# A streaming-encoder step on one core: the top-k rounds of the index attention as one list, 76 ahead of the first attention unit and 134 behind the reciprocals of group a's units

## The reference

```
shift, scale, gate = split(silu(c) @ w_ada + b_ada)
h = x * (1 + scale) + shift
qa, ka, va, ga, qb, kb, vb, gb, qi, ki, wi = split(h @ w_in)
oa = sliding-window attention(qa, ka, va, sinks, bias)            # group a, 16 heads
score = sum over 8 heads of relu(qi . ki / 8) * wi / sqrt(8)
idx = top_k(score, 256)                                           # 144 for the sample
ob = attention(qb, kb, vb) over the keys idx alone                # group b, 16 heads
y = concat(oa * silu(ga), ob * silu(gb)) @ w_out
out = LayerNorm(ALPHA * x + gate * y)
```

## Time and profile before

| | |
|---|---|
| median of 3 runs | 2170.78 us (2169.03 to 2174.48) |
| the profiled execution's own time | 2169.62 us |
| its span, first to last instruction | 2167.5 us |
| mean granted TensorE clock | 0.967 |
| busy share of the span | PE 92%, PEld 73%, DVE 45%, ACT 33%, POOL 28% |
| chain that ended last, by engine | PE 75%, DVE 10%, DMA 4%, ACT 4%, issue 3% |

### The profile page before, as it was taken

How to read it: one execution, slowest core, us unless ns; L and a number is a source line. 1 busy time by engine, 2 the same in 40 slices (tenths; PEclk the granted TensorE clock), 3 DMA queues, 4 the chain that set the end, 5 groups by cost and what they waited for, 6 DMA issues and landing times.

```text
span 2167.5 us, 34153 instructions
## 1 busy us (share of the span) xinstructions
PE 2003.6 (92%) x13111; PEld 1586.1 (73%) x13111; DVE 974.4 (45%) x2446; ACT 705.0 (33%) x1522; POOL 601.9 (28%) x607
## 2 busy tenths in 40 slices
PE   6889999959999999999899999999998889999991
PEld 3567789848888887888677777777776568777770
DVE  2433468876667776512223232232334422122447
ACT  2244422113233323333343434334435522221112
POOL 0331111112222222222222222222222434433333
PEclk8899999979999999999999999999999999999996
DMA  9943113312222222222211111111114134553443
GB/s 342 361 161 112 26 47 85 91 39 62 77 74 75 57 77 72 77 52 65 50 25 41 40 25 41 40 25 40 25 41 164 44 98 128 146 153 112 130 155 98
DMA packets 249922, 193.84 MB, mean 89 GB/s; under 512 B 149393, under 2 KB 202897, under 8 KB 247969
## 3 DMA queue, kind: packets, MB, share of 16 engines
q1 hardware_dynamic: 233072, 174.94, 28.2%
q10 hardware_dynamic: 15616, 12.49, 1.8%
q0 software_dynamic: 1072, 4.24, 0.6%
HBM read 171.28 MB, written 24.53 MB: 90 GB/s over the span
## 4 chain that ended last, share of the span: by engine, by line
PE 75%; DVE 10%; DMA 4%; ACT 4%; issue 3%; POOL 2%; SPq 1%; DVEq 0%; POOLq 0%; ACTq 0%
PE psum L1619 12%; PE psum L1621 10%; PE psum L1620 10%; PE psum L1697 6%; PE psum L1718 6%; PE psum L1719 5%; PE psum L1720 5%; PE psum L1655 5%; PE psum L1675 5%; DVE room L1202 4%; DVE room L1199 3%; DMA ada_ring<-in_w_ada_dram 2%; PE psum L1590 2%; PE psum L1546 2%; DMA w_raw<-in_w_out_dram 1%
## 5 line engine op out<-in xcount | busy, mean ns | idle before, releaser
L1619 PE MATMUL psum<-h_hi,w_hi 128*128 128x364 f32 (+1 forms) x1536 | 552.3, 360 | 6.7 <-issue 3.6
L1621 PE MATMUL psum<-h_lo,w_hi 128*128 128x364 f32 (+1 forms) x1536 | 507.2, 330 | 0.0
L1620 PE MATMUL psum<-h_hi,w_lo 128*128 128x364 f32 (+1 forms) x1536 | 504.2, 328 | 0.0
L1619 PEld LDWEIGHTS psum<-h_hi,w_hi 128*128 128x128 f32 x1536 | 290.3, 189 | 101.5 <-issue 96.1
L1081 POOL TENSOR_SCALAR room<-room 128x256 f32<-128x256 f32 (+9 forms) x252 | 149.0, 595 | 642.1 <-DVE room L1301 641.8
L1620 PEld LDWEIGHTS psum<-h_hi,w_lo 128*128 128x128 f32 x1536 | 292.2, 190 | 0.0
L1621 PEld LDWEIGHTS psum<-h_lo,w_hi 128*128 128x128 f32 x1536 | 290.3, 189 | 0.0
L1066 POOL TENSOR_TENSOR w_lo<-w_raw,w_hi 128x512 fp32r<-128x512 f32 x128 | 164.8, 1287 | 331.6 <-ACT w_hi L872 331.6
L1718 PE MATMUL psum<-w_hi,h_hi 128*64 128x512 f32 (+1 forms) x576 | 231.2, 401 | 14.1 <-POOL w_lo L1071 10.2
L1071 POOL TENSOR_TENSOR w_lo<-w_raw,w_hi 128x512 fp32r<-128x512 f32 x128 | 172.5, 1348 | 234.6 <-ACT w_hi L879 234.6
L1719 PE MATMUL psum<-w_lo,h_hi 128*64 128x512 f32 (+1 forms) x576 | 226.4, 393 | 0.0
(11 more groups left out here) (164 smaller groups left out, 2668.0 us busy)
## 6 DMA issues: line engine op xcount, KB each, us to landing
ada_ring<-in_w_ada_dram SPq DMA_DIRECT2D x64, 512.0 KB, 9.3
w_raw<-in_w_in_dram SPq DMA_DIRECT2D x256, 128.0 KB, 2.5
w_raw<-in_w_out_dram SPq DMA_DIRECT2D x256, 128.0 KB, 2.9
w_raw<-in_w_ada_dram SPq DMA_DIRECT2D x128, 128.0 KB, 2.1
x_rows<-in_x_prompt_dram SPq DMA_DIRECT2D x8, 1024.0 KB, 12.5
w_raw<-in_w_in_dram SPq DMA_DIRECT2D x32, 256.0 KB, 2.8
room<-in_x_prompt_dram SPq DMA_DIRECT2D x8, 1024.0 KB, 8.3
mix_transposed<-room SPq DMA_DIRECT2D x14, 544.0 KB, 3.0
```

Of the source, the lines that this page charges most:

```text
L1619: pe.matmul(Z, w_hi, hh[:, k, a:b], start=(k == 0), stop=False)
L1620: pe.matmul(Z, w_lo, hh[:, k, a:b], start=False, stop=False)
L1621: ins = pe.matmul(Z, w_hi, hl[:, k, a:b], start=False, stop=(k == KT - 1))
```

## The change

The two lists of rounds become one, `K_ROUNDS`, in the order of the tiles. 76 of its rounds run ahead of the first unit: all of tiles 2 and 3, and 12 of tile 4's. The other 134 are dealt out by `rounds_at(u)` over units 0 to 67: two to each unit, but one to units 33 and 67. All of a unit's rounds now stand behind its two reciprocals; none stands between the gate and the reciprocals any more. A tile's mask still follows its last round, and `mask_ready` follows the last round of all.

```diff
-K_EARLY = [2, 3, 4]
-K_LATE = [t for t in (5, 6, 7, 8) for _ in range((TOPK_P if t < NTILE - 1 else TOPK_S) // 8)]
-K_STEP = 2
+K_ROUNDS = [t for t in range(2, NTILE) for _ in range((TOPK_P if t < NTILE - 1 else TOPK_S) // 8)]
+K_EARLY = 76
+
+
+def rounds_at(u):
+
+    n, last = len(K_ROUNDS) - K_EARLY, 8 * STEPS - 4
+    return min(n, -(-n * (u + 1) // last)) - min(n, -(-n * u // last))
...
-        for t in K_EARLY:
-            for _ in range(TOPK_P // 8):
-                topk_round(t)
-            mask_of(t)
+        rounds = [0]
+
+        def topk_some(n):
+            for _ in range(n):
+                t = K_ROUNDS[rounds[0]]
+                topk_round(t)
+                rounds[0] += 1
+                if rounds[0] == len(K_ROUNDS) or K_ROUNDS[rounds[0]] != t:
+                    mask_of(t)
+                if rounds[0] == len(K_ROUNDS):
+                    dve.sem_inc(mask_ready.sem, 1)
+
+        topk_some(K_EARLY)
...
             shift_a(u)
             if u >= 2:
                 gate(u - 2)
-            topk_some(K_STEP // 2)
             denominator(u, 0)
             denominator(u, 1)
-            topk_some(K_STEP - K_STEP // 2)
+            topk_some(rounds_at(u))
```

## The result

The changed kernel takes 2179.5 us (median), the kernel before 2170.1 us in the same comparison: a ratio of 1.0049, 95% interval 1.0034 to 1.0065. It is slower by half a percent, where 2178.2 us was predicted.

A forecast was written before the change was run, and what follows sets the result against it. PE's work plus its waits bound the kernel; on the profiled 2169.62 us, -24.7 - 2.5 + 15.0 + 5.7 + 2.0 + 11.9 = +7.4 gives 2177.0, with the median 1.2 above: 2178.2 us; range 2162 to 2190 us.

The forecast's parts named there:

- The early list: Ahead of unit 0: 20 fewer early rounds remove PE's wait on DVE, -24.7 us, and its half-clock tail, -2.5 us.
- Step 4: Behind step 4's late second reciprocal, PE's p.v waits 2p - 2.32 (p: one round); sum 17.0 us, +15.0 over before.
- Step 1: At step 1, lateness from step 0 delays `shift_a`, gate, SP's store and load, so PE's gate row waits longer: +5.7 us.
- Steps 2 and 3: In PE's short units, rounds of 896 and 1024 keys may leave waits: 0 to 4 us, taken as +2.
- The clock: After eight of twelve waits at step 1 and behind step 4, TensorE's clock drops; seven more than before, +11.9 us.
- The clock holds: Rival, chance 0.17: waits come as worked out, but none to three are followed by the lower clock; 2164.6 to 2170 us.
- DVE's lateness doesn't reach PE: Rival, chance 0.12 wholly or half: the early wait goes and p.v finds its gate in time; 2141.6 us, half 2160.
- A wait takes the early one's place: Rival, chance 0.11: something hidden holds unit 0, or DVE lags from unit to unit in 1024-key units; lasting lag 2194 us.

The follow-up runs named there:

- the busy matmuls: The changed kernel plus 116 matmuls whose result nobody reads, put where PE waits at steps 5 and 1; 2166.25 us, 0.9979 of the kernel before.
- the store behind the loads: The changed kernel with SP's store of the pair before put behind the two gate weight loads; 2144.63 us, 0.9883 of the kernel before.
- step 4 alone: The changed kernel with both rounds ahead of the reciprocals in the eight units of step 4 only; 2166.45 us, 0.9989 of the kernel before.
- the placement undone: The changed kernel, 76 rounds still early, with one round of each unit ahead of its reciprocals and one behind; 2140.95 us, 0.9865 of the kernel before.

## Why the prediction was right, step by step

- **The early list, -24.7 and -2.5.** Right. The wait is gone, the next thing that could have been late (ACT's eviction, keys, tables) was not, and unit 0 runs at 1.00 from its first matmul: its q.k takes 0.49 us instead of 0.80. The two kernels with one round on either side that differ only in the list, 76 and 90, lie 17.6 us apart; 12.5 us of it is the wait, the rest the clock's tail and what the runs vary by.
- **Step 4, 2p - 2.32, 17.0 in sum.** Right in place and form. Measured behind step 4: 1.29, 1.85, 1.83, 2.39, 2.36, 2.90, 2.93 and 0.78 us in the eight pairs, 16.3 in sum, against 1.50, 1.96, 1.96, 2.50, 2.50, 3.04, 3.10 and 0.42. All but the last are 0.1 to 0.2 less than predicted. In unit 31 the reason is that two rounds before a `shift_a` take 4.72 us (703.49 to 708.21), not two times 2.41: `shift_a` starts at 708.21, before the last MATCH_REPLACE8 ends at 708.30. The last is 0.4 more, as in pair 7 the second reciprocal starts 1.09 us behind PE's unit and PE wants p.v 4.33 us into it, where the rule took 0.87 and 4.54 from pair 3. Of the 2.0 us of such waits before, 0.7 is in group b, so step 4 grew by 15.0 us, as forecast.
- **Step 1, +5.7.** The sum is right, 6.2. Unit 9's part is not: 3.24 - 1.43 = 1.8 us late instead of 0.7. Its mask took 1.52 us where the estimate allowed 0.8 with all around it; the last section says why. The other five are 0.2 to 1.7 more than before against 0.35 to 1.43 predicted.
- **Steps 2 and 3, +2.** Right: 18.9 - 16.3 leaves 2.6 us in seven waits; six of them, 1.8 us, stand behind steps 2 and 3 in the units of 896 and 1024 keys, and one of 0.7 in group b.
- **The clock, +11.9 with eight drops.** Right in the median run: keeping PE busy is worth 13 us. The profiled execution has more: 15.4 us of busy time in group a, where 11.9 less the 2.5 of the early tail was forecast, and 4.3 us outside it that no term of the sum covers. These 6.0 and 4.3 us cover what lies between its 2186.0 us and the 2177.0 reckoned for such an execution; its waits in group a, 23.0 us more against 22.7, came as forecast. The runs of this one kernel spread from 2175.45 to 2189.23 us. The count of drops was a choice between two bounds; that the forecast meets the median within 1.3 us is partly luck.
- **The rivals.** "The clock holds" fell by the busy matmuls and by the ten waits, none over 3.3 us, with 0.50 beside them. The Trainium skill ("TensorE: Matmul & The Clock Gate", section "HAM oscillation — how this bites in real kernels") warns of gaps longer than all of these; this trace does not agree with that bound. "DVE's lateness doesn't reach PE" fell by the 18.9 us. "A wait takes the early one's place" did not come about: no lag builds up from pair to pair, since at step 6 of every pair `shift_a` waits for PE again, 0.78 to 4.21 us.

What the prediction did not see is how much was open beside the change: the placement hid a gain of 30 us, and a store ahead of two loads cost 16 us (2140.95 against 2124.61), by waits that the kernel before has as well.

## What to carry to other kernels

Work that an engine does in its spare time belongs where that engine waits, not behind what it waits for: behind the reciprocals of step 4 each round made the next unit's p.v late by its full length, ahead of them one round was free, and a second one made POOL and the transposes late. To price such a move, take the unit in which the wait ends latest, and follow it to the engine that sets the end; eight units of 72 carried 16.3 of the 18.9 us of p.v's waits. The queue here held a store that waits for compute, and it delayed the loads behind it; so put the loads that the busy engine needs ahead of it.

## What the runs showed of the hardware that was not expected

**A mask that stood still behind POOL.** The mask over 640 keys takes 0.49 us on DVE in the kernel before, where POOL is idle. In the kernel after it took 1.52 us, at the end of unit 9. POOL's and DVE's timelines there:

```profile
520.11 1.29 POOL L1071 TENSOR_TENSOR w_lo<-w_raw,w_hi 128x512 fp32r<-128x512 f32 x1 [2.99 <-ACT w_hi L877]
```

```profile
520.23 1.52 DVE L1218 TENSOR_SCALAR room<-room 128x640 bf16<-128x640 f32 x1
```

POOL's instruction began 0.12 us earlier and ended at 521.40; the mask ended at 521.75, about a third of a microsecond later. The busy matmuls, the store behind the loads and step 4 alone have the same two at the same distance, and the mask takes 1.51 or 1.52 us in each. With the order the other way round, the mask over 768 keys kept its 0.56 us while POOL started 0.27 us after it, and POOL's took 1.44 us instead of 1.29:

```profile
655.94 0.56 DVE L1218 TENSOR_SCALAR room<-room 128x768 bf16<-128x768 f32 x1
...
656.21 1.44 POOL L1071 TENSOR_TENSOR w_lo<-w_raw,w_hi 128x512 fp32r<-128x512 f32 x1 [3.81 <-ACT w_hi L877]
```

In both orders the later one lost 0.14 us less than the two overlapped: 1.03 of 1.17 us, and 0.15 of 0.29. Where the two don't overlap (the placement undone) the 640 mask took 0.50 us. The Trainium skill ("SBUF — State Buffer", section "Who interferes with whom") says that the two engines share a pair of ports, and that whoever starts first keeps it for the whole instruction, for DVE's faster modes. The rows agree in who stood still. That the waiting took place at the ports is the Trainium skill's reading; no row shows it.

**Short waits cost the clock.** In the kernel after ten of the eleven waits of PE of 1.8 to 3.3 us have at least 3.4 us at 1.2 GHz beside them, so each of the ten cost some 1.5 us or more beside its own length (half of the busy time in the stretch). 116 useless matmuls in those waits won 13 us. The length of a wait alone does not decide it: with the store behind the loads, p.v waits 1.86, 1.83 and 2.39 us at the places where the kernel after waits 1.85, 1.83 and 2.39 us and the clock falls, but there it stays at 1.00. In that kernel the gate row's waits between these are gone; that this is the reason is not shown.
